# Where eight loads of modulation weights are requested: behind the last expert weights, or behind the combining stage's fourth gather

## The reference

```python
# first block, per layer: 32 experts, two per token, rows sorted into blocks
xb = h[row_tok].reshape(n_blocks, MOE_BLOCK, D)
def expert_block(args):
    xe, e = args
    return (jax.nn.silu(xe @ w1[e]) * (xe @ w3[e])) @ w2[e]
yb = lax.map(expert_block, (xb, block_e)).reshape(n_rows, D)
y = jnp.zeros((T, D), jnp.float32).at[row_tok].add(yb.astype(jnp.float32) * row_gate[:, None])
...
h = _layer_norm(DN_ALPHA * h + ff, ln2_g[li], ln2_b[li])
...
# second block: six modulation vectors of width D, one product with w_mod
m_lat = (jax.nn.silu(c) @ w_mod[l] + b_mod[l]).reshape(B_, 1, N_MOD, D)
m_ctx = (jax.nn.silu(c_ctx) @ w_mod[l] + b_mod[l]).reshape(N_MOD, D)
```

## Time and profile before

| | |
|---|---|
| median of 3 timed runs | 3542.68 us (3539.8 to 3544.4) |
| profiled execution, first to last instruction (its own time; nothing else is reported around it) | 3543.4 us |
| busy share: PE, PE weight loads, DVE, ACT, POOL | 88%, 67%, 50%, 25%, 15% |
| first layer: last weights requested, combining starts on PE, combining ends | 1033.30, 1049.55, 1095.51 us |
| second layer: the same | 2068.88, 2085.32, 2129.33 us |

### The profile page before, as it was taken

The page is one execution under the profiler, slowest core; times in us unless marked ns, Lnnn a source line. Parts: engine busy times, 40 slices in busy tenths (PEclk is TensorE's granted clock), DMA queues, the critical chain, the costliest instruction groups (busy, mean ns, idle before and its releaser), DMA issues. The chain is left out here.

```text
span 3543.4 us, 71427 instructions
## 1 busy us (share of the span) xinstructions
PE 3115.3 (88%) x30014; PEld 2390.6 (67%) x30014; DVE 1760.2 (50%) x3252; ACT 886.8 (25%) x1900; POOL 522.3 (15%) x807
## 2 busy tenths in 40 slices
PE   6899899958767998999958768899988899999999
PEld 3676799735435775888735434566656688878888
DVE  3445466441114444565441135355468776577742
ACT  3123233031113123333031132233354211022211
POOL 0000454001110001553011110000045300000000
PEclk9998699979987997899979978999999999999999
DMA  7110300259985101201189983110010122222221
GB/s 245 41 36 28 145 5 5 84 204 367 403 320 161 42 18 73 102 5 41 47 306 390 403 292 125 38 36 25 19 55 13 48 84 72 95 71 84 92 81 42
DMA packets 171523, 419.98 MB, mean 119 GB/s; under 512 B 30113, under 2 KB 116513, under 8 KB 145745
## 3 DMA queue, kind: packets, MB, share of 16 engines
q1 hardware_dynamic: 152241, 381.49, 29.1%
q0 software_dynamic: 8736, 17.32, 2.0%
q10 hardware_dynamic: 10240, 16.79, 1.5%
HBM read 398.82 MB, written 50.54 MB: 127 GB/s over the span
## 5 line engine op out<-in xcount | busy, mean ns | idle before, releaser
L2144 PE MATMUL ps<-e_w,e_xt 128*64 128x256 f32 x1792 | 229.6, 413 | 68.9 <-DMA e_w<-in_moe_w 67.5
L2144 PEld LDWEIGHTS ps<-e_w,e_xt 128*64 128x64 f32 x1792 | 151.7, 150 | 167.9 <-issue 79.2
L775 PE MATMUL ps<-h,win 128*128 128x264 f32 x960 | 229.8, 394 | 16.2 <-DVE pad L944 14.6
L2251 DVE TENSOR_TENSOR e_hid<-ps,e_silu 64x256 f32<-64x256 f32 x64 | 39.4, 616 | 394.1 <-ACT e_silu L2210 394.1
L775 PEld LDWEIGHTS ps<-h,win 128*128 128x128 f32 x960 | 183.0, 193 | 52.9 <-issue 21.9
L1525 DVE COPY_PREDICATED inv<-level,ps 112x384 f32<-112x384 int32 x176 | 103.5, 588 | 85.2 <-PE ps L1437 76.8
L3675 PE MATMUL ps<-h_lat,wt 128*128 128x256 f32 x528 | 127.7, 384 | 6.7 <-ACT h_lat L3812 6.5
L1437 PE MATMUL ps<-inv,nt 48*48 48x48 f32 x3520 | 126.0, 210 | 5.5 <-issue 3.9
L3675 PE MATMUL ps<-h_lat,w_sums 128*128 128x256 f32 x544 | 130.7, 384 | 0.0
L2163 PE MATMUL ps<-e_w,e_hid_t 128*64 128x512 f32 x448 | 112.9, 623 | 15.0 <-DMA e_w<-in_moe_w 10.4
L1364 ACT ACTIVATE nt<-ps 112x192 f32<-112x192 f32 x220 | 72.7, 330 | 183.5 <-PE ps L1426 176.4
(11 more groups left out here) (664 smaller groups left out, 6824.5 us busy)
## 6 DMA issues: line engine op xcount, KB each, us to landing
e_w<-in_moe_w SPq DMA_DIRECT2D x168, 1024.0 KB, 13.8
early<-in_moe_w SPq DMA_DIRECT2D x24, 1024.0 KB, 13.0
wt<-in_w_up SPq DMA_DIRECT2D x22, 1024.0 KB, 4.9
y_rows<-e_y ACTq DMA_DIRECT2D x128, 128.0 KB
win<-in_w_in SPq DMA_DIRECT2D x10, 1536.0 KB, 6.8
wmod<-in_w_mod SPq DMA_DIRECT2D x24, 512.0 KB, 15.3
wt<-in_w_in SPq DMA_DIRECT2D x11, 1024.0 KB, 4.9
early<-in_w_mod SPq DMA_DIRECT2D x16, 512.0 KB, 11.1
```

The costliest lines, as they stand in the source:

```text
L775: last = pe.matmul(ps[:, 7, 0:HT], lhsT=ring[(s + 1) % 2][:, i, o:o + P], rhs=k.h[:, i, h * HT:(h + 1) * HT], start=(i == 0), stop=(i == K ...
L2144: last = pe.matmul(ps[half, 2 + z, 0:EH], lhsT=xt[z][:, f, :], rhs=w[:, f, :], start=(f == 0), stop=(f == KD - 1))
L2251: dve.tensor_tensor(hid[z][high, :].rearrange("s (t q) -> s q t", t=2), ps[high, 2 + z, 0:EH].rearrange("s (q t) -> s q t", t=2), si[z][hi ...
```

## The change

The eight calls of `load_mod` leave the combining stage's SP program and stand at the end of the expert stage's SP program. The tiles, the sizes, the order among the eight and what waits for them stay. `load_mla` keeps its wait for the fourth gather and is now the first request of its stage.

```diff
             z, c = in_loop(n_turns, -3)
             load_down(1, owner[0:1, bass.ds(n_turns * 2 + (AHEAD - 1), 1)], (z, c))
+            for i in range(KD):
+                load_mod(k, a, li, sp, i)
...
         def _(sp):
             sp.wait_ge(landed[3], 32)
-            for i in range(KD):
-                load_mod(k, a, li, sp, i)
             load_mla(k, a, sp, li * -1 + LAYERS - 1)
             for landed_w in (k.win_mla, k.win_rest):
                 sp.wait_ge(landed_w, 32)
```

## The result

The changed kernel takes 3548.31 us (median of 19 runs, 3540.16 to 3556.32), the kernel before 3540.94 us (19 runs, 3533.46 to 3545.42). The ratio is 1.0024, 95% interval 1.0015 to 1.0032: 5 to 11 us slower, some 8.5 us. The forecast was +6.2 us.

A forecast was written before the change was run, and what follows sets the result against it. The expert stage's end was taken to hang on the last pair of stores. Two layers at +3.7 us, less 1.2 in the first, gave +6.2 on 3542.68, given as 3549.0 us; range 3541.5 to 3551.5, far end 3554.5.

The forecast's parts named there:

- the last copy would wait for `y_rows`: Sign at each layer's expert stage end: the last copy of line 2260 waits for stores, about 1 us late.
- the DMA rate would be near 400 GB/s without a pause: Sign at the expert stage's end: DMA rate near 400 GB/s from 1038 to about 1050 with no pause.
- the last pair would land only when the loads are nearly through: Expert stage's end: last pair lands at 1051.2, against 1047.5 before; loads stop at about 1050.1.
- at 21.2 us or more (not halved): Sign against the forecast: last weight request to combining's first PE work, 16.25 us before, about 20 forecast, reaches 21.2 or more.
- The hold-up: Expert stage's end: 512 KB loads delay a store pair 2.9 us, half of 5.8 beside weights; it needs 5.6, alone 2.7.
- The last pair: Expert stage's end, each layer: the last pair of stores lands 3.7 us late, and barrier and combining stage follow.
- the loads' end: Expert stage's end: eight loads and two store pairs, 4.7 MB at 400 GB/s, take 11.8 us from about 1038.3 to 1050.1.
- the hold-up is not halved: Rival, expert stage's end: pair lands 8.5 us after its request, +5.0 us per layer, +8.8 in all, 3551.5 us; chance 0.25.
- the 0.2% that I called the limit: About 0.2%, or 7.1 us, is what a measurement of this kernel can tell from no change; slower beyond it: chance 0.38.
- Combining: Combining stage: waits for the loads vanish, winning 1.2 us in the first layer (bounds 0 to 2.4), nothing in the second.
- SP's wait at the stage's end: Combining stage's end: SP's wait for the `load_mla` pairs, 7.2 us before, becomes shorter; it hides and is worth nothing.

The follow-up runs named there:

- 1024 KB: Against the changed kernel: four unused expert-weight loads of 1024 KB replace the eight loads, which return behind the fourth gather; run once, +4.9 us by stages against before.
- requests alone: Against the changed kernel: the eight early requests carry 8 KB each, the real loads return behind the fourth gather; run once, -2.6 us by stages against before.

## Why the prediction was right, and where it was off

**Mechanism: right, and shown.** The loss sits at the end of the expert stage, once per layer, because the last stores land late beside the loads. With the bytes taken away and the requests kept, it is gone. That the last copy would wait for `y_rows`, that the DMA rate would be near 400 GB/s without a pause, and that the last pair would land only when the loads are nearly through all stand in the rows. The size, though, is that of a rival: of the signs that the prediction named, the distance "at 21.2 us or more (not halved)" is the one that came, with 21.4 and 21.5 us. And that the measured 3548.31 us lies so near the forecast 3549.0 is luck: the forecast was added to 3542.68 us, and the kernel before took 3540.94 beside the changed one.

**The hold-up: mis-sized.** The step "the modulation loads are of 512 KB, half of it, so I take half, 2.9 us: a pair needs 5.6 us" failed. The pair took 7.4 us (hold-up 4.7), the copy was 2.9 late and not 1.1. The reason for halving was wrong: with 256, 512 and 1024 KB per request the pair took about 7, 7.4 and 8 us. What it left out is that no byte of the pair moves for the first 4 us. The rule of the Trainium skill weighed there (DMA: Bandwidth & Descriptors, Queues, rings and completion order: an engine turns between queues in packets of typically 9 to 17 descriptors) was used to say that two loads of 512 KB may go in one turn, as one of 1024 KB, so that the time does not halve. Read evenly it does not say so: by the prediction's own count a load of 128 rows leaves eight rows on each DMA engine whatever its size, so a turn would hold as many rows of 2, 4 or 8 KB, and the hold-up would double from size to size. The measured hold-ups (4.4, 4.7 and 5.0 us in the first layers) do not, and the measurement decides.

**The last pair: 3.7 us forecast, 5.1 and 5.0 measured.** This is the term that makes up the miss. I put the loads' end 1050.1 - 1033.30 = 16.8 us after the last weight request, from 400 GB/s to the last byte. They ended at 1039.3, 18.6 us after 1020.69. By 1038, 17.3 us, the engines had moved 363 to 419 GB/s and nearly all was through; the last 0.08 MB of loads took 1.3 us more, while the busy share of the DMA engines fell to 0.22. PE's first work follows the loads' end by 2.8 us (1042.08 - 1039.3), where the forecast had some 3.1 (1.1 to the pair's landing and 2 from there). 1.8 us less 0.3 make up the miss of 1.4 within their rounding. Per layer the price is that of the rival "the hold-up is not halved" (5.0), and so is the sum: +8.1 by stages against that rival's +8.8 and the forecast's +6.2. The measured 8.5 us lie above the 0.2% that I called the limit, with an interval that reaches below it.

**Combining: -1.2 us in the first layer, as forecast, but not shown to come from the loads.** From the turning of chunk 2 to the end it took 16.8 us before and 15.65 after. In the second layer I expected nothing and it won 1.1 us as well (15.6 to 14.55, of which 0.3 was lost ahead of it). No load wait was there to remove. The rows show the clock instead: windows of the second layer from the turning of chunk 2, before:

```profile
2113.00:2118.00 5.00, 4.30 (x28) 3.01 (x32) 4.00 (x7) 3.58 (x8) 0.00 (x0) 0.50 1.03 409
2118.00:2129.30 11.30, 7.88 (x96) 4.79 (x88) 10.15 (x29) 7.53 (x22) 0.00 (x0) 0.80 0.67 227
```

and after:

```profile
2110.00:2115.00 5.00, 4.14 (x32) 3.06 (x36) 4.00 (x7) 3.75 (x8) 0.00 (x0) 0.56 0.72 225
2115.00:2125.40 10.40, 6.48 (x92) 4.00 (x84) 10.12 (x29) 7.66 (x22) 0.00 (x0) 0.96 0.00 0
```

The granted clock rises from 0.50 (1.2 GHz) to 1.00 (2.4 GHz) during the products, earlier after than before. With two loads early, while the other six still move beside it (326 to 414 GB/s in each of the first nine us of the first layer's stretch in the untimed run), that stretch took 14.56 us in both layers of one execution and 14.56 and 16.0 in those of the other, with no wait for a load in either. So neither load waits nor the transfers beside the stretch make this difference, and up to 1.5 us of such a stage belongs to no load. That it is the clock's phase is read from these rows and was not tested. The forecast took its 1.2 us from one execution, as if the second layer's 15.6 were the time without waits and the first layer's 16.8 the time with them. In the two runs with all eight modulation loads in their old place and the same work around them the stretch took 15.43 and 15.5 us (requests alone) and 14.98 and 15.08 (1024 KB), with waits for the loads of 0.74, none, 0.28 and 0.23: all below 16.8, and the first below the changed kernel's 15.65. So the waits' price is not known, and that the forecast 1.2 us came out in this profile is luck as far as these runs go.

**SP's wait at the stage's end** became longer (8.5 for 7.2 us), where I had said shorter. It costs nothing: the requests now end at 1067.3, so the wait is over near 1075.8, eleven us before ACT's last work ends.

**What the runs say of the hold-up.** One reading fits them: a pair lands with the loads' last bytes, give or take 1 us, or some 6 to 8 us after its request, whichever is first. Two loads end early enough to hide in the 4.5 us that the copy can bear; four hold the first pair but free the last; eight hold both; sixteen add only 1.3 to 2.1 us to the measure over eight. This was formed from the runs; I did not test it by one of its own. About 4 us of the 7 to 8 pass before the held pair's first byte moves, with 256, 512 and 1024 KB per request alike. Why that is so stays open, and so does whether being ahead in the same queue protects a store.

## What to carry to other kernels

A stretch in which the DMA engines look idle is not free when the only transfers in it are stores that end the stage: what counts is the landing of the last store, and 4.2 MB of loads beside it cost 5 us per layer, for a gain of at most about 1 that the runs do not tell from scatter. Read first how many us a store can bear before somebody waits (here 4.5 for one pair, none for the last), and place only as many bytes as are through by then: two of the eight loads cost nothing. To price a hold-up, look for a loaded store in the trace and take its full time; scaling it by the size of the neighbouring requests was the error here. A gain read off one execution needs a second one before it goes into a sum.

## What the runs showed of the hardware that was not expected

A pair of stores of 128 KB takes 2.7 us alone and 6.8 to 8.2 us beside loads, nearly whatever the size (256 to 1024 KB) and number (four to sixteen) of the loads. Beside eight loads its first byte moves some 4 us after the request, alone 1.1. Four loads requested on SP in the same moment as a pair of stores on ACT still make the pair's stage end 3.5 us later. Eight requests of ACT take 4.46 us of ACT, which ends the stage 2.9 us later when ACT is what the barrier waits for; on SP the same eight cost nothing.
